# Attention start: merged, re-laid-out loads on two queues, no mask matmul, stores on ScalarE's queue

## The reference

```python
def sb_block(q_blk, q_start, k, v, bias):
    valid = k_pos[None, :] < q_pos[:, None]                 # strictly causal
    z = jnp.einsum('bqhd,bkhd->bhqk', q_blk, k) + bias[None, :, None, None]
    lneg = jnp.where(valid, jax.nn.log_sigmoid(-z), 0.0)
    suffix = lax.cumsum(lneg, axis=3, reverse=True) - lneg  # of the keys behind s
    w = jnp.where(valid, jnp.exp(jax.nn.log_sigmoid(z) + suffix), 0.0)
    return jnp.einsum('bhqk,bkhd->bqhd', w, v)
# run_trunk: h += gla_mixer(rmsnorm(h)); kv = rmsnorm(h) @ w_kv; proj = rmsnorm(h) @ w_in_b
#            o = sb_attention(q, keys, vals, bias) * silu(gate); h += o @ w_out_b; rmsnorm(h, g_final)
```

## Time and profile before

| | us |
|---|---|
| median of 3 runs | 3365.58 (3365.28 to 3365.92) |
| the profiled execution | 3368.11 |
| its span from first to last instruction | 3366.5 |
| PE busy | 3155.3 (94%) |
| DVE busy | 1661.5 (49%) |
| ACT busy | 1399.5 (42%) |
| POOL busy | 889.0 (26%) |

### The profile page before, as it was taken

How to read it: one execution, slowest core, us unless ns; L and a number is a source line. 1 busy time by engine, 2 the same in 40 slices (tenths; PEclk the granted TensorE clock), 3 DMA queues, 4 the chain that set the end, 5 groups by cost and what they waited for, 6 DMA issues and landing times. The chain is left out here.

```text
span 3366.5 us, 49760 instructions
## 1 busy us (share of the span) xinstructions
PE 3155.3 (94%) x17836; PEld 2474.9 (74%) x17836; DVE 1661.5 (49%) x1967; ACT 1399.5 (42%) x2332; POOL 889.0 (26%) x936
## 2 busy tenths in 40 slices
PE   6999999799799799999999499999999999799998
PEld 6999999556588699999999355555555555466665
DVE  5111122387544411222222388998899897443442
ACT  5111111265311211112211278888888787344442
POOL 0000000254111000000000266776677675100000
PEclk8999999799899899999999699999999999899999
DMA  4122111455255421444431555343433410999995
GB/s 152 62 71 76 69 57 58 159 187 182 103 183 178 147 76 51 176 170 147 165 101 57 137 151 142 79 123 107 119 88 103 123 36 16 354 325 374 366 339 210
DMA packets 257393, 489.74 MB, mean 145 GB/s; under 512 B 27133, under 2 KB 142562, under 8 KB 245922
## 3 DMA queue, kind: packets, MB, share of 16 engines
q1 hardware_dynamic: 232450, 350.61, 32.3%
q0 software_dynamic: 24752, 136.63, 11.3%
HBM read 329.58 MB, written 157.59 MB: 145 GB/s over the span
## 5 line engine op out<-in xcount | busy, mean ns | idle before, releaser
L1736 POOL TENSOR_TENSOR att_w<-att_w,att_rest 128x1023 f32<-128x1023 f32 (+7 forms) x384 | 615.4, 1606 | 303.0 <-DVE att_rest L1703 289.9
L470 PE MATMUL projb_acc<-projb_x_hi,projb_w_hi 128*128 128x416 f32 x1280 | 451.0, 352 | 16.5 <-DVE projb_w_lo L452 16.5
L470 PE MATMUL projb_acc<-projb_x_hi,projb_w_lo 128*128 128x416 f32 x1280 | 449.2, 351 | 0.0
L470 PE MATMUL projb_acc<-projb_x_lo,projb_w_hi 128*128 128x416 f32 x1280 | 448.9, 351 | 0.0
L1564 PEld LDWEIGHTS att_wT_acc<-const_ident,att_w 128*128 128x128 f32 x2176 | 236.9, 142 | 210.2 <-issue 152.9
L1653 ACT ACTIVATE att_rest<-att_z,att_bias 128x1024 f32<-128x1024 f32 (+7 forms) x384 | 333.3, 868 | 85.4 <-PE att_z L1610 55.5
L1703 DVE TENSOR_TENSOR_SCAN att_rest<-att_rest,att_zero 128x128 f32<-128x128 f32 (+7 forms) x256 | 355.0, 1402 | 23.2 <-ACT att_rest L1653 23.1
L292 PE MATMUL proja_acc<-proja_x_hi,proja_w_hi 128*128 128x416 f32 x1000 | 353.7, 354 | 0.8 <-DVE proja_x_lo L265 0.7
L292 PE MATMUL proja_acc<-proja_x_hi,proja_w_lo 128*128 128x416 f32 x1000 | 351.8, 352 | 0.0
L292 PE MATMUL proja_acc<-proja_x_lo,proja_w_hi 128*128 128x416 f32 x1000 | 350.0, 350 | 0.0
L1564 PE MATMUL att_wT_acc<-const_ident,att_w 128*128 128x128 f32 x2176 | 314.9, 281 | 31.2 <-ACT att_k_tok L1668 14.8
(11 more groups left out here) (256 smaller groups left out, 4910.4 us busy)
## 6 DMA issues: line engine op xcount, KB each, us to landing
smp_k_pages<-in_cache_k SPq DMA_DIRECT2D x128, 512.0 KB, 7.2
smp_v_pages<-in_cache_v SPq DMA_DIRECT2D x128, 512.0 KB, 7.2
proj_b<-projb_out POOLq DMA_DIRECT2D x32, 1040.0 KB, 4.4
proj_a<-proja_out POOLq DMA_DIRECT2D x24, 1040.0 KB, 4.5
kq_hi<-early_area POOLq DMA_DIRECT2D x16, 1024.0 KB, 6.0
kq_lo<-early_area POOLq DMA_DIRECT2D x16, 1024.0 KB, 8.9
att_q_hi<-kq_hi SPq DMA_DIRECT2D x60, 256.0 KB, 4.1
att_q_lo<-kq_lo SPq DMA_DIRECT2D x60, 256.0 KB, 5.1
```

The source lines that it names most:

```text
L470: mm = pe.matmul(acc[:, q, 0:size], w[:, b, k, :], x[:, k, at:at + size], start=(k == 0 and w is w_hi and x is x_hi), stop=(k == KD - 1 an ...
L1736: pool.tensor_tensor(these, these, passed[:, 1:size], ALU.mult).then_inc(w_made, 1)
```

## The change

- Attention: the mask matmul and `diag_mask` go. In their place the scan of a not carried item starts at 0 and adds a tile `begin`, zero but for an identity in its last 128 columns: the product becomes 1 at the diagonal and stays 0 right of it. `begin` is a PSUM bank of 1024 bf16, cleared by DVE and filled by one transpose of PE. POOL multiplies the whole item instead of all but its last column.
- Layout: keys and queries are stored as `k_parts` and `q_parts`, by pair, 512 tokens, part, channel, head, token. A load of keys is then one DMA of 128 partitions with 4 KB each (2 MB for a later pair instead of eight DMAs of 256 KB), a load of queries for 512 tokens four DMAs of 64 partitions with 4 KB each. The high part lies always in the lower half of the partitions.
- Start of `att`: ACT's queue issues keys 0, bias, keys 2 and keys 1 of pair 0. SP's queue issues the queries, raw keys and values and the gate. Queries are no longer loaded in pieces of 128 and 384 tokens.
- Turns of pair 0 move from beats 7, 8, 9, 10 to 6, 8, 10, 12, and a value product waits for its own turn only.
- `proja` and `projb`: the stores move from POOL's queue to ACT's, which waits for the copies and gate products itself. Parts are stored with 4 DMAs per block instead of 2.
- `proja` and `outa`: the table of ACT that holds the square root is loaded at once.
- `gla`: SP loads `gate_weights(1)` ahead of `early.load`.

```diff
+            act.preload_act_table_set("sqrt_and_others")        # proja, outa
...
+                act.wait_ge(gain_in, 32)                         # proja, ACT, after the 5 evictions
+                act.dma_start(dst[ds(n * P, width), :], out[0:width, b, :]).then_inc(stored[b], 16)
...
+                    to = parts[j].rearrange("a u e p h n -> e h p (a u) n")   # projb, ACT
+                    for part, made in enumerate((high, low)):
+                        for h in range(2):
+                            act.dma_start(to[part, h, :, ds(jb * NCH, NCH), :], ...).then_inc(parts_stored, 16)
...
-            early.load(sp)
             sp.wait_ge(logit_cp, 5)
             gate_weights(1)
+            early.load(sp)
...
-            put(7 + m if pair == 0 else 40 * (pair - 1) + LAG + 1 + 2 * m, ("turn", pair, m))
+            put(6 + 2 * m if pair == 0 else 40 * (pair - 1) + LAG + 1 + 2 * m, ("turn", pair, m))
...
             def load_k(pair):
-                for u in range(NCH):
-                    load_k_span(pair, u, 0, 4, in_k[pair % 2])
+                sp.dma_start(k2[:, pair % 2, :, :, :], k_parts[pair].rearrange("u e p h n -> (e p) u (h n)")
+                             ).then_inc(in_k[pair % 2], 16)
...
-                if j == 4 * g + 3:
-                    pe.wait_ge(copied[1], turn_end[pair])
+                if j % 4 == 3:
+                    pe.wait_ge(copied[1], ring_no["turn", pair, j // 4] + 1)
...
-                if not carried:
-                    pe.matmul(z_ps[:, n % 2, size - P:size], c.ident_bf[:, :], c.diag_mask[:, :], start=True,
-                              stop=False, skip_group_check=True)
...
+            pe.transpose(begin[:, 1024 - P:1024], c.ident_bf[:, :], c.ident_bf[:, :]).then_inc(begin_made, 1)
...
+                    else:
+                        dve.tensor_tensor_scan(passing, passing, begin[:, 1024 - size:1024][:, ::-1],
+                                               rest[:, n % n_rest, 1024:1025], ALU.mult, ALU.add).then_inc(scanned, 1)
```

More of the change, by code:

```diff
@@ L324, in _ @@
             over_blocks(pe, step)
-        @block.gpsimd
-        def _(pool):
-            def store(n, i, b, width, gate, follows_gate):
-                if gate:
-                    pool.wait_ge(gate_made, (n - first_gate) * n_spans + n_spans)
-                else:
-                    pool.wait_ge(copied, n * n_spans + n_spans)
-                pool.wait_ge(gain_in, 32)
-                pool.dma_start(dst[ds(n * P, width), :], out[0:width, b, :]).then_inc(stored[b], 16)
-            store(0, 0, 0, P, False, False)
-            over_blocks(pool, store)
-            pool.wait_ge(stored[0], 16 * (blocks // 2 + 1))
-            pool.wait_ge(stored[1], 16 * (blocks // 2))
 def project(nc, c, name, xnT, jobs, parts, early):
@@ L1383, in prompt_attention @@
     k_rows, v_rows, g_rows = 0, D, 3 * D
-    k_parts, q_parts = 0, D
+    k_parts, q_parts = parts
     order = attention_schedule()
@@ L1479, in load_q @@
                     for half in range(2):
-                        sp.dma_start(dst[half * HD:(half + 1) * HD, g, :, :],
-                                     head_rows(part, q_parts + pair * P)[:, :, g * BANK:(g + 1) * BANK]
-                                     ).then_inc(in_q[g], 16)
+                        sp.dma_start(dst[half * HD:(half + 1) * HD, g, :, :], q_parts[pair, g, part]).then_inc(in_q[g], 16)
             def load_raw(pair, m):
@@ L1728, in _ @@
                     n, size = z_no[(kind, pair, *x)], hi - lo
-                    passed = rest[:, n % n_rest, 1024 - size:1024]
+                    passed = rest[:, n % n_rest, 1024 - size:1025]
+                    n_passed = size - 1 if carried else size
                     pool.wait_ge(sig_made, n + 1)
@@ L1734, in _ @@
                     pool.wait_ge(scanned, n + 1)
-                    these = weight(pair, phase, h, t, 0, size - 1)
-                    pool.tensor_tensor(these, these, passed[:, 1:size], ALU.mult).then_inc(w_made, 1)
+                    these = weight(pair, phase, h, t, 0, n_passed)
+                    pool.tensor_tensor(these, these, passed[:, 1:n_passed + 1], ALU.mult).then_inc(w_made, 1)
                     if lo:
```

138 lines of the change are left out of this document (61 added, 77 removed).

## The result

The changed kernel takes 3331.18 us (median of 4 runs, 3327.94 to 3331.77), the kernel before 3365.75 in the same session (3365.28 to 3370.68), a ratio of 0.9892 with a 95% interval from 0.9875 to 0.9909. The forecast was 3324 with a range from 3308 to 3341. The time lies in the range, but the start and the turns of the first pair together gave a quarter of their 17 us, the stores gave eight times their 1.0, and the sum hid it.

What follows compares the result with a forecast made beforehand. PE, or what PE waits for, was taken to bound the kernel nearly everywhere. Terms 17 + 8 + 9 + 3.3 + 2.6 - 0.7 + 1.0 = 40.2 us gave 3325.4, with 1 us for the clock 3324; range 3308 to 3341.

Steps and rivals of the forecast that it cites:

- Mask, 17 us: Attention: dropping 256 mask matmuls of at most 0.10 us each gains 2.1 us per pair, 17 us in all.
- Scan with `begin`, 0: Attention's 256 not carried scans on DVE: reading a full bf16 row from PSUM costs nothing extra; bounds 0 and double time.
- The rival that the scan pays: Attention scans slow down by reading `begin`; at half as much again the kernel takes 3425 us; chance 0.06.
- Start of the attention, 8 us: First pair: merged loads on two queues start "below" 5 to 10 us earlier; 8 us taken as gain.
- 3 MB take 9 us: Start of attention: queries and keys 0 and 2 transfer at the last stage's 333 GB/s, from 1880 to 1889.
- The slow bound: Start of attention: the same 3 MB take 14 us at the present start's 208 GB/s, so "below" starts at 1909.
- 20.6 us of issue against 14 us of transfer: Start of attention: SP's 32 DMA issues outlast 4.8 MB at 333 GB/s, so a second queue was held to help.
- Turns of the first pair, 9 us: First pair: wider beats cut ACT's 16.7 us of waits for `k_tok`'s store to 7.7, gaining 9 us.
- the rival that transfers decide the first pair: First pair: loads run no faster, start and turns give 5 us instead of 17, time 3336; chance 0.15.
- `gla`, 3.3 us: Stage `gla`: head 1's gate weights ahead of 3 MB arrive 8 us before needed, removing PE's 3.26 us wait.
- Tables, 2.6 and -0.7: ACT's early table load gains 2.6 us at the first stage's start and loses about 0.7 in `outa`.
- Stores, 1.0 us: Projection stores on ACT's queue: 0.5 us gained at each of two stage ends, no cost to PE; bounds 0 and 2.

Runs made afterwards that it cites:

- e1: Changed kernel with the mask matmul put back and the scans' start as before: 3343.8 us.
- e6: Changed kernel with the first pair's turns one beat apart again, at beats 7 to 10: 3326.6 us.
- e5: Changed kernel with the first pair's keys 0, 2, 1 and the bias back on SP's queue, one queue for the first loads: 3329.2 us.
- e10: Changed kernel with small first query loads, keys 1 later, `k_tok`'s store ahead of a turn's loads, and turns of pairs 0 and 1 moved later: 3312.9 us.
- e3: Changed kernel with the 3 MB of output weights in `gla` issued ahead of head 1's gate weights again: 3335.2 us.
- e11: Kernel before with one edit, the stores of both projections issued by ACT's queue in the old layout: 3356.5 us.
- e8: Changed kernel with keys 1 issued by SP behind the raw keys and values, not by ACT ahead of all: 3330.5 us.
- e9: Changed kernel with pair 1's four turns at beats 24, 26, 28, 30 instead of 12, 14, 16, 18: 3323.1 us.
- e2: Changed kernel with the stores of both projections issued by POOL's queue again, in the new layout: 3338.0 us.

## Why the prediction was right in the sum and wrong in its parts

- **Mask, 17 us.** The mechanism was right (e1), the size some 13: 1.98 per period, 11.0 at pair 7. It overstated pairs 0 and 1, where PE was waiting anyway. In the three phases of pair 3 the forecast hit 2.1 with 2.09, but by luck: "first" and "middle" gave 1.42 of up to 2.4, and "above" 0.67 where I had counted 0.2.
- **Scan with `begin`, 0.** Right. 128 columns 465 ns and 1024 columns 2339, against 464 and 2337 in the earlier trace rows. The rival that the scan pays is refuted.
- **Start of the attention, 8 us.** Wrong by its own mark, "below" 5 to 10 us earlier: 0.2 with turn 0 inside, 1.4 with the turn behind (e6). The step that failed is "3 MB take 9 us" at 333 GB/s. Tile 8 came at 18.1 us, after 4.16 MB at 230 GB/s. Both factors were off. I had counted only the bytes that the first tiles want, as if the queues would send those first, when the other 1.2 MB were in flight beside them; and I had taken the rate of a stage in full flow. The slow bound that I had worked out (208 GB/s, 14 us) was the nearer one and still 4 us short. What I said of the stretch behind tile 8 held: 1.2 + 3.8 + 10.2 = 15.2 us, and in e6 it is 15.2 (18.2 to 33.4). I dismissed the Trainium skill's rule ("DMA: Bandwidth & Descriptors", Issuing engines are not separate DMA queues) with 20.6 us of issue against 14 us of transfer. e5 sides with the rule: with four more issues on SP "below" comes 3.2 us earlier, so the issue wasn't the limit once the loads were merged.
- **Where the start did pay.** e6 has all edits of the attention but the turns' beats. At pair 7 it is 19.0 us ahead of before, of which the mask explains 11.0 (e1): 8.0 are left for loads and layout, the very figure of the forecast, but at another place and so by chance. In e6 turn 0 of pair 1 comes at 63.4 us instead of 68.6, without the wait of 4.40 us for the store.
- **Turns of the first pair, 9 us.** Wrong in sign: -3.6 (e6). The step that failed is the subtraction in "Now it's four beats, about 12 us at 3 us per beat", which takes the store's landing as given. The beats came out: from the copies of turns 0 and 1 to where ACT stood ready for those of turns 2 and 3 it is 10.3 and 14.0 us. But that wasn't enough. From a copy to the landing of its store it took 14.0, 20.4 and 19.2 us (turns 0, 1 and 2), against 13.9, 17.5 and 17.0 before, and the waits still sum to 16.6. Start and turns together gave 4.3 us (769.7 to 765.4 at pair 7 between before and e1, which differ in them and not in the mask), near the 5 of the rival that transfers decide the first pair. That rival said that the loads run no faster, though, and they do (229 against 143 GB/s in the first 18 us); and with the bytes asked for at other times e10 takes 18.2 us out of the same pair.
- **`gla`, 3.3 us.** That the 3 MB in flight make PE wait was right, that the weights would be there 8 us before was not: they are issued as late as ever and land sooner (e3). The size was too small, 4.4 to 6.5. I had named the clock behind the pause as "a few us more" and left it out of the term.
- **Tables, 2.6 and -0.7.** Right for the first product, 2.6 us; at the stage's end 0.7 to 3.3, by where the clock falls. In `outa` the loss is there too: PE is idle for 14.83 us before its first matmul instead of 14.23 (14.80 to 14.90 in all eleven traces with the early load, 14.05 and 14.23 without), so -0.6. In the table above it lies inside the 6.5 us of `gla`.
- **Stores, 1.0 us.** The largest miss upwards: 2.9 + 5.6 = 8.5 us in this trace, 9.0 by e11's time. I had taken 0.5 per stage end from the issue alone (0.53) and had the gap itself in the trace, from 1868.35 to 1879.22, 10.9 us of which the transfer explains 4.2, and didn't ask what the remainder was. That ACT's stores cost PE nothing was right.

Against the forecast's terms start and turns gave 13 us less, the mask 4 less, the stores 7.5 more and `gla` 3 to 4 more; the tables gave 2 less, and some 3 us more lie in rows that single traces don't resolve. That the total came within 4 us of the 40.2 is largely luck.

## What to carry to other kernels

Before pricing a schedule, look at whether the DMA engines are full in each stretch, and whether they stand idle in one just ahead. Where they are full, spreading or closing up the waits, reordering and a second queue mostly moved the wait to another name (e5 to e8: 0.1 to 3.5 us at pair 2), and more came from bytes wanted later (e9, 6.1) or moved earlier into the idle stretch (e10, 18.2 with all edits). What goes out on a second queue isn't free even when it issues for nothing: it takes bandwidth from what is wanted first. Check a forecast part by part, since a sum can be right by cancelling. And read the still time at the end of each stage, from the last landing to the next stage's first instruction, as a term of its own.

## What the runs showed of the hardware

- A stage whose last store went out from POOL's queue, and whose landing POOL awaited, ended 3.6 and 6.7 us after the landing (3.1 and 4.0 in e2), one with ACT 1.0 and 1.4 us (landings after 2.8 and 4.2, and 2.6 and 3.9 us; from issue to the next load 6.4 and 10.9, and 3.6 and 5.3).
- A scan on DVE with a second stream in bf16 from PSUM takes as long as one with a broadcast number: 465 ns against 464 for 128 columns, 2339 against 2337 for 1024.
- The first 18 us of `att` moved 143 GB/s in short pieces from one queue, 229 merged on two queues and 270 merged on one (e5), where the last stage moves 333.
- A load of 8 KB landed 1.5 us after its issue with nothing large ahead of it, and 10.5 us after it behind 3 MB on the same queue.
- Behind a pause of 2.85 us PE ran at 1.2 GHz for some 6 us, though busy throughout (0.67 over 10 us). By an estimate from that, 6 us at half speed, 3 us were lost on top of the pause.
- A bf16 matmul of 128x128 ahead of the logits, 221 ns in its row, held up the attention by 62 ns on average, 34 to 109 by phase.
